# A first overflow block in two parts: its gather and gate-up behind the expert's own gate-up, its down and combine where the block stood

## What is computed

```python
top_logit, top_e = lax.top_k(logits, TOP_K)            # 4 of 32 experts for each of 256 tokens
top_w = jax.nn.softmax(top_logit, axis=-1)
...
gu = xb @ w_gu[e] + b_gu[e]                            # 1024 -> 2048
gate = jnp.minimum(gu[:, :D_EXPERT], 7.0)
up = jnp.clip(gu[:, D_EXPERT:], -7.0, 7.0)
act = gate * jax.nn.sigmoid(1.702 * gate) * (up + 1.0)
y = act @ w_dn[e] + b_dn[e]                            # 1024 -> 1024
...
out = jnp.zeros((T, D), h.dtype).at[buf_tok].add(ys.reshape(P, D))
```

## Time and profile before

| | |
|---|---|
| median of three executions | 1132.6 us |
| span of the profiled execution | 1131.7 us |
| TensorE busy, share of the span | 94% |
| VectorE, ScalarE, GpSimd busy | 21%, 13%, 2% |
| read from HBM | 425.04 MB |
| mean rate over the span | 376 GB/s |

### The profile page before, as it was taken

One profiled execution on the slowest core, in us unless ns is written; L12 is line 12 of the kernel. 1 busy time (PEld: TensorE's weight loads), 2 busy tenths in 40 slices (PEclk: granted clock), 3 DMA queues, 4 the chain that ended last, 5 costly groups with the idle time before them and its releaser, 6 DMA issues.

```text
span 1131.7 us, 14828 instructions
## 1 busy us (share of the span) xinstructions
PE 1062.0 (94%) x5442; PEld 463.3 (41%) x5443; DVE 239.4 (21%) x734; ACT 151.1 (13%) x316; POOL 20.5 (2%) x49
## 2 busy tenths in 40 slices
PE   7999999989999999999999989999999999999895
PEld 6777644333534333333232323434333334343331
DVE  3354663201111111110111101111111111111014
ACT  2043611010101010100010100101010101010020
POOL 2000210000000000000000000000000000000000
PEclk9999999989999999999999989999999999999999
DMA  9723459969999999999999999999999999999993
GB/s 312 268 112 76 189 203 385 403 271 396 426 425 426 426 426 426 426 426 426 426 426 424 427 395 428 427 426 427 429 426 426 426 422 426 426 425 426 426 427 131
DMA packets 49412, 426.45 MB, mean 377 GB/s; under 512 B 5114, under 2 KB 9003, under 8 KB 16587
## 3 DMA queue, kind: packets, MB, share of 16 engines
q1 hardware_dynamic: 48666, 425.37, 90.9%
q10 hardware_dynamic: 720, 0.74, 0.2%
HBM read 425.04 MB, written 1.05 MB: 376 GB/s over the span
## 4 chain that ended last, share of the span: by engine, by line
PE 63%; DMA 33%; DVE 2%; issue 1%; ACT 1%; SPq 0%; DVEq 0%
PE PB L789 60%; DMA WB<-in_w_down_dram 29%; DMA WB<-in_w_gate_up_dram 3%; PE PB L1164 1%; DMA X<-in_x_dram 0%; PE PB L796 0%; DVE S L1569 0%; PE PB L893 0%; DVE S L1825 0%; DVE S L1603 0%; DVE K L1816 0%; DVE X L1608 0%; PE PB L894 0%; PE PB L895 0%; DVE K L1586 0%
## 5 line engine op out<-in xcount | busy, mean ns | idle before, releaser
L789 PE MATMUL PB<-WB,S 128*64 128x512 f32 (+5 forms) x3456 | 757.5, 593 | 40.0 <-DMA WB<-in_w_down_dram 30.9
L789 PEld LDWEIGHTS PB<-WB,S 128*64 128x64 f32 (+2 forms) x3456 | 258.7, 139 | 517.4 <-issue 438.7
L1702 DVE TENSOR_SCALAR S<-PB 128x512 f32<-128x512 f32 (+1 forms) x34 | 23.5, 691 | 482.8 <-PE PB L789 482.8
L789 PE MATMUL PB<-S 32*64 32x512 f32 (+5 forms) x456 | 104.5, 588 | 1.5 <-ACT S L710 1.4
L714 ACT ACTIVATE S<-S 128x512 f32<-128x512 f32 x32 | 20.2, 630 | 471.8 <-DVE S L1702 471.8
L1744 DVE COPY S<-PB 64x512 f32<-64x512 f32 x31 | 21.2, 684 | 281.0 <-PE PB L789 281.0
L789 PEld LDWEIGHTS PB<-S,X 128*128 128x128 f32 x512 | 59.7, 192 | 12.6 <-issue 12.2
L789 PE MATMUL PB<-S,X 128*128 128x128 f32 x512 | 63.9, 278 | 0.1
L789 PE MATMUL PB<-S,WB 128*128 128x256 f32 (+2 forms) x336 | 60.1, 377 | 0.4 <-ACT S L548 0.4
L789 PEld LDWEIGHTS PB<-S 32*64 32x64 f32 (+5 forms) x456 | 30.9, 147 | 62.9 <-issue 58.8
L730 ACT ACTIVATE S<-PB 64x512 f32<-64x512 f32 x31 | 18.4, 593 | 249.1 <-PE PB L789 249.1
(11 more groups left out here) (214 smaller groups left out, 332.5 us busy)
## 6 DMA issues: line engine op xcount, KB each, us to landing
WB<-in_w_gate_up_dram SPq DMA_DIRECT2D x128, 2048.0 KB, 25.8
WB<-in_w_down_dram SPq DMA_DIRECT2D x128, 1024.0 KB, 21.9
WB<-in_w_in_dram SPq DMA_DIRECT2D x3, 2048.0 KB, 15.3
WB<-in_w_in_dram SPq DMA_DIRECT2D x1, 2144.0 KB, 10.3
WB<-in_w_in_dram SPq DMA_DIRECT2D x2, 1024.0 KB, 10.6
WB<-in_w_out_dram SPq DMA_DIRECT2D x2, 1024.0 KB, 10.3
WB<-in_w_out_dram SPq DMA_DIRECT2D x1, 2048.0 KB, 7.9
WB<-in_w_in_dram SPq DMA_DIRECT2D x1, 1040.0 KB, 12.2
```

What stands on the lines that cost most here:

```text
L789: return mm_(o, l, r, start=start, stop=stop, skip_group_check=True)
L1702: ts(g, gate, LIMIT, None, ALU.min).then_inc(s[g_ok], 1)
```

## The change

The first extra block of an expert is cut in two. Its **first part** (wait for its one-hots, gather, two transpositions, gate-up, bias) moves directly behind the expert's own gate-up. Its **second part** (six transpositions, down, combine) stands where the block stood. A second and any later block of the same expert follows there in one piece, in a loop that now starts at 1. So each of the four places in TensorE's code now has a block's instructions twice, and two or three branches where there was one. The gather of a block moves from bank 4 to bank 6, its gate-up from bank 6 to bank 7; bank 7 holds the outputs of the expert before, so the waits for their copies move ahead with it. On ScalarE the copies and the sigmoid of the first part follow the own sigmoid. VectorE's and SyncE's programs keep their order. The core of the diff:

```diff
@@ ScalarE @@
+            def first_extra_slots(t):
+                with act.If(extra_count(t) > 0):
+                    extra_slots()
+                    extra_sigmoid()
+                act.nop()
...
+                n = extra_count(t)
                 with act.If(n > 0):
+                    extra_act_copy()
+                    extra_outputs()
+                act.nop()
+                with act.If(n > 1):
+                    with act.Fori(1, n):
                         extra_slots()
                         extra_sigmoid()
                         extra_act_copy()
...
                 sigmoid(2 * i + 2)
+                first_extra_slots(2 * i + 1)
                 slots_to_sbuf(0, 6, 2 * i + 3)
@@ TensorE @@
+            def first_extra_gate_up(e, t, outputs_copied):
+
+                with pe.If(extra_count(t) > 0):
+                    pe.wait_ge(s["ysb_ok"], outputs_copied + 1)
+                    if not (isinstance(outputs_copied, int) and outputs_copied == 0):
+                        pe.wait_ge(s["ysb_dv"], outputs_copied)
+                    extra_gate_up(e)
+                pe.nop()
+
+            def extra_blocks(e, loaded, t, pb6_copied, copies):
+
+                n = extra_count(t)
+                with pe.If(n > 0):
+                    pe.wait_ge(s[pb6_copied], copies)
+                    extra_down(e, loaded)
+                pe.nop()
+                with pe.If(n > 1):
+                    with pe.Fori(1, n):
+                        pe.wait_ge(s["xyd"], pe.snap(xcount, min_val=1, max_val=96))
+                        extra_gate_up(e)
+                        extra_down(e, loaded)
                 pe.nop()
...
                 gate_up(1, i + 1, 2 * i + 2)
+                pe.wait_ge(s["ct_sb"], i + 1)
+                first_extra_gate_up(1, 2 * i + 1, 2 * i + 1)
                 pe.wait_ge(s["ohs"], i + 2)
-                pe.wait_ge(s["ct_sb"], i + 1)
                 gather(0, 6)
                 pe.wait_ge(s["g_ok"], 2 * i + 2)
                 gather(1, 4, range(2))
                 act_transposes(2 * i + 2)
                 gather(1, 4, range(2, 4))
-                extra_blocks(1, i + 1, 2 * i + 1, "xg_ok", 2 * i + 4, 2 * i + 1)
+                extra_blocks(1, i + 1, 2 * i + 1, "xg_ok", 2 * i + 3)
                 down(1, i + 1, 2 * i + 2)
 
                 pe.wait_ge(s["xg_ok"], 2 * i + 4)
                 gate_up(0, i + 2, 2 * i + 3)
+                first_extra_gate_up(0, 2 * i + 2, 2 * i + 2)
                 pe.wait_ge(s["ysb_ok"], 2 * i + 3)
```

More of the change, by code:

```diff
@@ L690, in extra_slots @@
                 act.wait_ge(s["xga"], xc)
-                act.activation(xrows, PB[4][:, 0:256], ACT.Copy).then_inc(s["xgs"], 1)
+                act.activation(xrows, PB[6][:, 0:256], ACT.Copy).then_inc(s["xgs"], 1)
                 act.wait_ge(s["xgt"], xc)
-                act.activation(yx[:, 0:KT * XSLOTS], PB[4][:, 256:512], ACT.Copy).then_inc(s["xxg"], 1)
+                act.activation(yx[:, 0:KT * XSLOTS], PB[6][:, 256:512], ACT.Copy).then_inc(s["xxg"], 1)
             def extra_sigmoid():
@@ L730, in expert_output, with extra_count @@
                 act.activation(ysb[64 * e:64 * e + 64, 1, :], PB[7][64:128, :], ACT.Copy).then_inc(s["ysb_ok"], 1)
+            def extra_count(t):
+                return act.value_load(nx[0:1, t:t + 1] if isinstance(t, int) else nx[0:1, bass.ds(t, 1)], min_val=0,
+                                      max_val=MAX_EXTRA)
+            def first_extra_slots(t):
[3 more added lines that the diff above has]
+                act.nop()
             def extra_blocks(t):
-                n = act.value_load(nx[0:1, t:t + 1] if isinstance(t, int) else nx[0:1, bass.ds(t, 1)], min_val=0,
-                                   max_val=MAX_EXTRA)
+                n = extra_count(t)
                 with act.If(n > 0):
-                    with act.Fori(0, n):
+                    extra_act_copy()
[3 more added lines that the diff above has]
+                    with act.Fori(1, n):
                         extra_slots()
@@ L744, in _ @@
             act.activation(CT[:, 0, :], PB[1][:, 0:P], ACT.Copy).then_inc(s["ysb_ok"], 1)
+            act.wait_ge(s["nx_ok"], 1)
             sigmoid(1)
-            act.wait_ge(s["nx_ok"], 1)
-            extra_blocks(0)
+            first_extra_slots(0)
             act_columns(5, 1)
             combine_weights(1)
+            extra_blocks(0)
             expert_output(0, 1)
@@ L1227, in extra_combine @@
                         mm(acc(b, h)[:, :], CTx[64 * h:64 * h + 64, b, :], yx[64 * h:64 * h + 64, :], False, False)
[L1229 to L1251, removed]
@@ new lines, in extra_count, with extra_gate_up, extra_down @@
+            def extra_count(t):
+                return pe.value_load(nx[0:1, t:t + 1] if isinstance(t, int) else nx[0:1, bass.ds(t, 1)], min_val=0,
+                                     max_val=MAX_EXTRA)
+            def extra_gate_up(e):
+                extra_gather()
+                for c in range(GU_CHUNKS):
+                    extra_gate_up_chunk(c, e).then_inc(s["xguc"], 1)
+                extra_gate_up_bias(e).then_inc(s["xgu"], 1)
+            def extra_down(e, loaded):
+                extra_act_transposes()
+                xc = pe.snap(xcount, min_val=1, max_val=96)
+                pe.wait_ge(s["xctd"], xc)
+                pe.wait_ge(s["xactT"], xc)
+                for c in range(DN_CHUNKS):
+                    pe.wait_ge(s_dnl[e][c], 16 * loaded)
+                    extra_down_chunk(c).then_inc(s["xdnc"], 1)
+                extra_combine()
@@ L1317, in _ @@
             gate_up_bias(1).then_inc(s["gu"], 1)
+            pe.wait_ge(s["ct_sb"], PAIRS + 1)
+            first_extra_gate_up(1, N_EXPERTS - 1, N_EXPERTS - 1)
             pe.wait_ge(s["xa"], 1 + 2 * TB)
```

20 lines of the change are left out of this document (11 added, 9 removed).

## The result

The changed kernel takes **1353.78 us** (median of four executions, 1344.18 to 1360.52) against 1132.29 of the kernel before beside it: a ratio of 1.1948, interval 1.1900 to 1.1996. The change costs 221 us. The forecast of 1136.0 and its range (up to 1168) are missed by a long way; that it would be slower was right, and the cause is the third case of the prediction, which was priced at 32 us.

A forecast was written before the change was run, and what follows sets the result against it. The prediction took the weight transfers, at 421 to 429 GB/s, as the bound. Its terms, -3.5 - 1.2 + 2.5 + 2.5 + 0.7 + 2.4 = +3.4 us, added to the median 1132.6, gave 1136.0; range 1127 to 1168.

The forecast's parts named there:

- the third case of the prediction: TensorE's loop no longer stays on the engine and is refetched every pair: 32 us, 1168 (1140 to 1210), chance 0.24.
- the likeliest case: TensorE's code is fetched about once, stalling where jumps land: 1136.0 us (1131 to 1144), chance 0.50.
- The cost per pair: In TensorE's refetched loop: stalls of 3.1 and 4.1 us ahead of two downs plus clock, 9.3 on average.
- The reserve: TensorE's spare time against the weight transfers, 59.1 against 52.10 us per pair: 7.0 us per pair.
- the faster case: The code stalls don't come and both block gains stay: -5.6 us, 1127.0 (1125 to 1130), chance 0.22.
- Block 1: First overflow block, expert 1: earlier gate-up and down bring the next down load forward, -3.5 us (-1.7 to -5.2).
- Block 2: Second overflow block, expert 17: at most its own loss of 2.2 us returns; taken as -1.2 (-2.2 to -0.3).
- Expert 0's down at 203.1: Expert 0's down waits for a later instruction packet, starting at 203.1 instead of 200.62: +2.5 us (0 to 4).
- the jump over the loop copy of expert 1: Behind expert 1's block, the jump lands just ahead of a missing piece of code: +2.5 us (0 to 6).
- expert 2's down: The jump ahead of it crosses two code pieces, a 4.1 us stall; +0.7 at the end (zero or 3).
- The last expert: The jump ahead of its down lands where the next code piece is missing: +2.4 us (-1.3 to +3.2).

The follow-up runs named there:

- the shifted kernel: The changed kernel with 66 more instructions ahead of TensorE's loop, 60 of them never run, against the kernel before: 1136.47 us, ratio 1.0015.

## Why the prediction was wrong

**The step that failed is the choice between the cases.** The loop's place was counted right (11.84 to 18.45 by hand, 11.90 to 18.48 in the program; eight pieces and the next, nine), and the 8 blocks on TensorE that the prediction worked out from the Trainium skill (Runtime: NRT & Kernel Launch, Instruction fetch mechanics) are what the runs show: 7 and one behind run from the store, 8 and one behind don't. With both in hand the refetched loop got 0.24 and the loop that fits 0.50. The reason given against it, that nothing is refetched today with 7 pieces in use, is no evidence about 9. And the likeliest case allowed one new piece at each back jump, which is no state that any run shows: it is all or nothing, 126 packets in 14 pairs or none. The mechanism itself was stated right (each fetch throws out the next piece needed), and over 100 packets were named as its sign; so was a pair of over 59 us as the sign of being wrong, and it takes 70.4.

**The second is the price of that case**, +32 against +221. Two terms were mis-sized:

- The cost per pair was put at 9.3 us: two stalls of 3.1 and 4.1 and about 2 of clock. Measured: (185.6 - 40.6 + 35.2 of former waits for weights) / 14 = 12.9 of stalls, in four places and not two, and 62.9 / 14 = 4.5 of clock, together 17.4. The stalls ahead of the downs were 4.2 and 5.1 in the mean. Two places were left out: the loop's back jump (1.4), which the prediction names for its likeliest case but doesn't price in this one, and the gate-up behind it (2.3), where no jump lands. The clock was put at less than half.
- The reserve was put at 7.0 us per pair, the difference of two paces, over all 14 pairs. But TensorE waited for weights only 35.2 us in these pairs, 2.5 each. Behind a block it is behind the transfers and catches up at 52 us per pair with no wait at all; only where the pair takes 59 is there a reserve. The reserve is the idle time that the trace shows, not a difference of rates times the number of rounds. 17.4 - 2.5 is 14.9 per pair, and times 14 that is the 207.9 again (the same windows, so no check). With 9.3 and 2.5 the prediction would have had +95 for this case: still too little, but no longer near the others.

**The other terms**, read where the loop fits, in the shifted kernel (the faster case took 2.1 for block 2 where its bound was 2.2; nothing hangs on it):

- Block 1: the gate-up was put at about 230 and starts at 230.31, and the down at full clock takes 3.64, as assumed. But from the end of the own bias (226.25 + 1.09) to the end of the block's down (244.13 + 3.64) are 20.4 us, where before there were 26.6: 6.2 us gained and not 3.5, beyond the bound of 5.2. 1.7 of the difference is the block's gate-up, 7.07 at full clock where 8.77 was kept; the rest is shorter waits ahead of gate-up and down.
- Block 2: all of the loss comes back (395 to 426 GB/s), -2.2 and not -1.2, since no piece is fetched anew there.
- Expert 0's down at 203.1: it starts at 203.50. The size was right, but for half the reason: the packet would have made it so alone, and so would the table load, which the prediction didn't see. It had read the order of ScalarE's copies and not where the table load falls.
- Behind the jump over the loop copy of expert 1: 5.33 us instead of 2.5, near the upper end, and 1.4 more of clock in the down behind it (the down load came 3.63 us behind the start of its down instead of 2.20). Ahead of expert 2's down: 5.17 instead of 4.1.
- The last expert: +2.4 was forecast, and there is no stall at all: the last down starts behind 0.69 us of waiting for ScalarE, as it did before. Since the 1.30 us and the clock behind it are gone too, the stretch from the last transposes (1112.47) to the end is 1.9 shorter than before (21.8 against 23.8), beyond the bound of -1.3. In the kernel after itself a stall of 2.62 stands there and the stretch takes 25.5. Where a jump lands in pieces decides this, and 66 instructions ahead of it move it.

With these sizes the sum is: the down load behind block 1 at 259.43 instead of 255.56, less 0.3 by which that run began later, +3.6; +1.7 where expert 2's down comes after the queue has run dry (its load at 292.63, the queue empty at 259.43 + 2.0 + 29.5 = 290.9, an estimate); -2.2 at block 2; -1.9 at the end: +1.2. Forecast was +3.4. Measured is +3.3 by the medians, +1.7 by the ratio (-1.0 to +4.4) and +2.6 by the spans of the two profiled executions, of which 1.4 stays without a place. That the shifted kernel came out at the forecast 1136 was luck: block 1 gained 2.7 more than was summed and the end 4.3 more, and the stall behind block 1, its clock and expert 2's down cost more.

## What to carry to other kernels

Where a loop's code is larger than before, count its instructions and its place in pieces of the size of a code packet, and take "the loop and the piece behind it don't fit" as a case of its own, with all pieces fetched in every round: it is all or nothing, and 66 more instructions ahead of the loop can decide it. Price a new stall in a loop against the idle time that the trace really shows on that engine, not against a difference of rates. Where a copy of code is needed only for rare inputs, fold it into the common one (a loop that skips its first half once) before paying for two; and where an activation gets a second wait ahead of it, look at where its table load falls.

## What the runs showed of the hardware

- TensorE's code comes in packets of 16 KB (2.41 MB in 147). At 256 instructions each, which is the prediction's estimate from about 250, the places fit the packets of every kernel. A loop in 7 pieces and the next: 18 to 21 packets for the whole kernel. A loop in 8 and the next: nine per pair, ten where it lies in 9. A difference of 168 instructions in the loop (1509 to 1677), or of 66 in where it starts, made 1134 or 1136 us into 1354 or 1355.
- Ahead of the downs, behind a jump into code that isn't there, TensorE stood 4.2 to 6.8 us in the mean of 14 pairs (7.6 at most). 280 more or fewer skipped instructions changed that by 1.5 to 1.8 us, for more than a whole packet of 256. At expert 0's down 2.7 us lay between the packet and the first matmul.
- Behind such stalls the granted clock was 0.69 to 0.71 in the mean of the next 5.5 to 9.9 us. TensorE's busy time for the same 3750 matmuls grew by 62.9 us from 758, a third of the time lost, at a mean clock of 0.92 instead of 1.00.
- The load of ScalarE's function table takes 1.28 us. It ran at 182.08, ahead of the sigmoid's wait for its input, where the sigmoid had one wait ahead of it, and at 198.18, behind that wait, where it had two.
